# Three edits joined: the opening's group products, the index page transfers and samples' scores, and the last norm

## The reference

```
h = rmsnorm(x, g) * (1 + scale) + shift          # shift, scale, gate = silu(c) @ W + b
x = x + gate * f(h)
```

```
diff = mean_w(h) - h ;  f(h) = (diff @ w_grp[g]) * scale      # w_grp[g] is 256 x 256
```

## Time and profile before

| | us |
|---|---|
| three timed runs | 2660.32, 2654.61, 2649.01 |
| median | 2654.61 |
| the profiled execution, its own time | 2652.98 |
| its span in the trace | 2651.3 |
| busy: TensorE | 2385.3 (90%) |
| busy: VectorE | 1169.5 (44%) |
| busy: ScalarE | 679.7 (26%) |
| busy: GpSimd | 612.6 (23%) |
| opening | 0 to 166.4 |
| first FFN | 166.4 to 947.6 |
| attention input up to the end of the scores | 947.6 to 1134.4 |
| top-k search to second FFN | 1134.4 to 2612.8 |
| last norm | 2612.8 to 2651.3 |

### The profile page before, as it was taken

The page is one execution under the profiler, slowest core; times in us unless marked ns, Lnnn a source line. Parts: engine busy times, 40 slices in busy tenths (PEclk is TensorE's granted clock), DMA queues, the critical chain, the costliest instruction groups (busy, mean ns, idle before and its releaser), DMA issues. The chain is left out here.

```text
span 2651.3 us, 39897 instructions
## 1 busy us (share of the span) xinstructions
PE 2385.3 (90%) x14954; PEld 2064.6 (78%) x14954; DVE 1169.5 (44%) x2611; ACT 679.7 (26%) x1182; POOL 612.6 (23%) x447
## 2 busy tenths in 40 slices
PE   3589999999999998599979995688999999999994
PEld 2569999999999964166634442387999999999994
DVE  6746333333333352478737641233733333333336
ACT  2233111111111042478247761122311111111101
POOL 3602112222222004210036653130222222211210
PEclk8789999999999999799979997789999999999997
DMA  9441111111111032063130008611111111111101
GB/s 397 171 165 48 48 48 47 47 47 47 47 47 47 0 125 87 27 224 99 37 106 21 13 1 281 232 64 48 49 48 48 47 47 47 47 47 47 47 0 65
DMA packets 65631, 206.56 MB, mean 78 GB/s; under 512 B 9572, under 2 KB 28548, under 8 KB 52996
## 3 DMA queue, kind: packets, MB, share of 16 engines
q1 hardware_dynamic: 55184, 183.20, 18.8%
q0 software_dynamic: 7920, 21.22, 2.4%
q10 hardware_dynamic: 2436, 0.92, 0.2%
HBM read 188.52 MB, written 16.13 MB: 77 GB/s over the span
## 5 line engine op out<-in xcount | busy, mean ns | idle before, releaser
L736 PE MATMUL ps<-f_hhi,f_whi 128*128 128x352 f32 x2112 | 682.6, 323 | 3.8 <-DVE f_hlo L295 3.6
L737 PE MATMUL ps<-f_hhi,f_wlo 128*128 128x352 f32 x2112 | 676.8, 320 | 0.0
L738 PE MATMUL ps<-f_hlo,f_whi 128*128 128x352 f32 x2112 | 676.5, 320 | 0.0
L706 POOL TENSOR_TENSOR f_wlo<-f_raw,f_whi 128x2048 fp32r<-128x2048 f32 x62 | 285.2, 4603 | 1224.8 <-ACT f_whi L665 1040.9
L80 DVE SCALAR_TENSOR_TENSOR xT<-ps,mod,xT 128x352 f32<-128x352 f32 (+1 forms) x576 | 327.9, 572 | 214.8 <-PE ps L758 121.4
L736 PEld LDWEIGHTS ps<-f_hhi,f_whi 128*128 128x128 f32 x2112 | 396.1, 188 | 7.9 <-DVE f_hlo L295 6.5
L737 PEld LDWEIGHTS ps<-f_hhi,f_wlo 128*128 128x128 f32 x2112 | 396.9, 188 | 0.0
L738 PEld LDWEIGHTS ps<-f_hlo,f_whi 128*128 128x128 f32 x2112 | 395.9, 187 | 0.0
L756 PE MATMUL ps<-f_ahi,f_whi 128*128 128x352 f32 x1056 | 340.6, 323 | 0.0
L757 PE MATMUL ps<-f_ahi,f_wlo 128*128 128x352 f32 x1056 | 338.3, 320 | 0.0
L758 PE MATMUL ps<-f_alo,f_whi 128*128 128x352 f32 x1056 | 338.1, 320 | 0.0
(11 more groups left out here) (315 smaller groups left out, 2892.9 us busy)
## 6 DMA issues: line engine op xcount, KB each, us to landing
f_raw<-in_ffn SPq DMA_DIRECT2D x66, 1024.0 KB, 4.8
ada_raw<-in_ada SPq DMA_DIRECT2D x18, 2048.0 KB, 11.7
sa_kv<-in_ckv POOLq DMA_DIRECT2D x54, 256.0 KB, 4.5
xT<-in_ada SPq DMA_DIRECT2D x12, 1024.0 KB, 5.3
sa_kv<-in_ckv SPq DMA_DIRECT2D x42, 256.0 KB, 4.7
ai_w<-in_win SPq DMA_DIRECT2D x9, 1024.0 KB, 7.0
xT<-in_ckv SPq DMA_DIRECT2D x23, 256.0 KB, 2.7
xT<-in_xT SPq DMA_DIRECT2D x8, 528.0 KB, 11.0
```

Source lines behind the costliest of these rows:

```text
L706: pool.tensor_tensor(wlo[:, a, :], raw[:, a % 2, :], whi[:, a, :].bitcast(F32), ALU.subtract).then_inc(w_lo, 1)
L736: pe.matmul(c.ps[:, bank, 0:CH], hi[:, k, side, :], hhi[:, k, col], start=(k == 0), stop=False)
L737: pe.matmul(c.ps[:, bank, 0:CH], lo[:, k, side, :], hhi[:, k, col], start=False, stop=False)
L738: last = pe.matmul(c.ps[:, bank, 0:CH], hi[:, k, side, :], hlo[:, k, col], start=False, stop=(k == KD - 1))
```

## The change

Three edits, independent of each other in the code.

1. **Opening.** The mixing products take the plain fp32 weights and differences: two products per bank instead of six, and no rounding and no low halves (`whi`, `wlo`, `dhi`, `dlo` are gone). `df` holds all eight tiles, of the prompt alone. GpSimd makes the samples' differences into `fs`, both tiles of a group in one instruction; TensorE mixes them after the fourth group in 16 products of 32 columns into bank 0, and VectorE adds them in one step for all tiles. `between` becomes [6, 7], [8 to 10], [11, 12], [13 to 17]. Variance, root and reciprocal go by chunk. GpSimd loads `invc` and `vec` first and waits for the last x tile before it issues the other loads; VectorE waits for each table separately.
2. **Index pages and samples' scores.** `load_index_pages` is written out: two page numbers are read, then two DMAs issued, with places in SBUF fixed at build time. SyncE takes parts 0, 2 and 4; GpSimd 1, 3 and 5, all before its small transfers; ScalarE 6 and 7, four pages after each of the evacuations n = 4 to 11, and then the three weight loads. The samples' scores come one at a time after chosen pairs of heads. VectorE's use of the small transfers moves to the last head of block i = 1.
3. **Last norm.** Squares, sums, variance, root and reciprocal by chunk, as in the attention input stage; VectorE makes six y tiles per chunk, GpSimd two (the product with g ahead, then the one with the inverse root); nine stores instead of eight.

The diff, cut to its core:

```diff
 def front_phase
-        between = [range(6, 7), range(7, 9), range(9, 12), range(12, 15), range(15, NQ)]
+        between = [range(6, 8), range(8, 11), range(11, 13), range(13, NQ)]
 ...
 scalar:
-            norm.act_std(act)
-            act.wait_ge(raw_ready, 16)
-            act.activation(whi[:, :], raw[:, :], ACT.Copy).then_inc(w_hi, 1)
+            for ch in range(NCH):
+                act.wait_ge(norm.var_ready, ch + 1)
+                act.activation(norm.rstd[:, cols(ch)], norm.rstd[:, cols(ch)], ACT.Sqrt).then_inc(norm.std_ready, 1)
 ...
-                    if j >= 2:
-                        act.wait_ge(mixed, 6 * g)
-                    act.wait_ge(s_diff, g + 1)
-                    act.wait_ge(scaled, j + 1)
-                    act.activation(dhi[:, j % 2, :], f, ACT.Copy).then_inc(d_hi, 1)
+                    act.activation(df[:, j, 0:SEQ], df[:, j, 0:SEQ], ACT.Copy, scale=c.mod[:, 0, KD + j, 0:1]).then_inc(scaled, 1)
 gpsimd:
+            pool.dma_start(c.invc[:], d.invc).then_inc(invc_ready, 16)
+            pool.dma_start(c.vec[:], d.vec).then_inc(vec_ready, 16)
+            pool.wait_ge(x_ready[KD - 1], 16)
 ...
-                for j in (2 * g, 2 * g + 1):
-                    pool.wait_ge(d_hi, j + 1)
-                    pool.tensor_tensor(dlo[:, j % 2, :], df[:, j % DF, :], dhi[:, j % 2, :].bitcast(F32), ALU.subtract).then_inc(d_lo, 1)
 tensor:
-                            pe.matmul(c.ps[:, q, 0:CH], hi[:, g, k, w], dhi[:, k, col], start=(k == 0), stop=False)
-                            pe.matmul(c.ps[:, q, 0:CH], lo[:, g, k, w], dhi[:, k, col], start=False, stop=False)
-                            last = pe.matmul(c.ps[:, q, 0:CH], hi[:, g, k, w], dlo[:, k, col], start=False, stop=(k == 1))
+                            last = pe.matmul(c.ps[:, q, 0:width(ch)], w[:, g, k, m * P:(m + 1) * P], df[:, 2 * g + k, prompt(ch)], start=(k == 0), stop=(k == 1))
+                if g == 3:
+                    pe.wait_ge(s_diff, 1)
+                    pe.wait_ge(added, 19)
+                    for j in range(KD):
+                        h, m = divmod(j, 2)
+                        for k in range(2):
+                            last = pe.matmul(c.ps[:, 0, NS * j:NS * (j + 1)], w[:, h, k, m * P:(m + 1) * P], fs[:, 2 * h + k].rearrange("p b t -> p (b t)"), start=(k == 0), stop=(k == 1))
+                    last.then_inc(s_mixed, 1)
 vector: (differences 0 to 3, modulation(0), differences 4 and 5, residuals(0), 6, residuals(1), 7, then)
+            residuals(2)
 ...
             modulation(1)
-            residuals(2)
             residuals(3)
+            sample_residuals()

 def load_index_pages
-    with pool.Fori((part % 2) * PAGES // 2, (part % 2 + 1) * PAGES // 2) as i:
-        for half in range(2):
-            page = pool.value_load(c.ptab[0:1, bass.ds(i + (2 * two + half) * PAGES, 1)], min_val=0, max_val=d.n_pages - 1)
-            pool.dma_start(...)
+    for n in range(first, last, 2):
+        i = (part % 2) * PAGES // 2 + n // 2
+        pages = [eng.value_load(...) for half in range(2)]
+        for half in range(2):
+            eng.dma_start(...)

 def attention_input_phase
-        between = [[], [0, 1], [2, 3], [4], [5, 6], [7, 8, 9]]
+        between = {(2, 0): 0, (2, 2): 1, (3, 0): 2, (3, 2): 3, (4, 0): 4, (4, 1): 5, (4, 2): 6, (5, 0): 7, (5, 1): 8, (5, 2): 9}
 sync:
-            sp.wait_ge(ready, EARLY)
-            for u in range(3, 6):
-                sp.dma_start(w[:, u % 3, :], d.win[ORDER[u]]).then_inc(w_ready[u % 3], 16)
-            for p in (4, 6, 7):
-                load_index_pages(sp, c, d, p, page_sp[1])
+            load_index_pages(sp, c, d, 4, page_sp[1])
 gpsimd:
+            load_index_pages(pool, c, d, 5, page_pool[1])      # ahead of the small transfers
 scalar, after evacuation n:
+                if n >= 4:
+                    for p in range(2):
+                        load_index_pages(act, c, d, 6 + p, page_act, max(PAGES // 4 * (n - 4) - PAGES * p, 0), min(PAGES // 4 * (n - 3) - PAGES * p, PAGES))
+            for u in range(3, 6):
+                act.dma_start(w[:, u % 3, :], d.win[ORDER[u]]).then_inc(w_ready[u % 3], 16)
 vector:
-                    if i == 1 and hd == 3:
+                    if i == 1 and hd == NIH - 1:
                         dve.wait_ge(smp_ready, 16 * 14)

 def final_phase
+        @block.gpsimd
+            for i in range(PT):                                 # PT = 2
+                pool.tensor_scalar(xg[:, i, :], c.xT[:, DT + i, :], c.vec[:, g0 + DT + i:g0 + DT + i + 1], None, ALU.mult).then_inc(g_ready, 1)
+            for ch in range(NCH):
+                pool.wait_ge(rstd_ready, ch + 1)
+                for i in range(PT):
+                    pool.tensor_tensor(y[:, DT + i, cols(ch)], xg[:, i, cols(ch)], rstd[:, cols(ch)], ALU.mult).then_inc(y_pool, 1)
 vector:
+            variance(0)
+            invert(0)
+            for ch in range(NCH):
+                tiles(ch, 0, 3)
+                if ch < 2:
+                    variance(ch + 1)
+                tiles(ch, 3, DT)                                # DT = 6
+                if ch < 2:
+                    invert(ch + 1)
```

More of the change, by code:

```diff
@@ L554, in link, with invert @@
                 dve.wait_ge(step, n[0])
+            def invert(ch):
+                dve.wait_ge(norm.std_ready, ch + 1)
+                dve.reciprocal(norm.rstd[:, cols(ch)], norm.rstd[:, cols(ch)]).then_inc(norm.rstd_ready, 1)
             def modulation(s):
@@ L1141, in _ @@
                     pe.matmul(c.ps[:, 2 * (n % 2) + a, 0:wd], qi[rows, j, BLK[i] * P:(BLK[i] + 1) * P], kst[rows, k0:k0 + wd], start=True, stop=True).then_inc(s_ready, 1)
[L1142 to L1144 removed]
+                if (i, j) in between and k0 + wd == widths[i]:
+                    sample_scores(between[i, j])
             head_sum(2 * (SKC + 1) - 1)
@@ L1960, in _, with squares, std @@
         @block.scalar
         def _(act):
-            norm.act_squares(act)
-            norm.act_std(act)
+            def squares(first, last):
+                for n in range(first, last):
+                    ch, j = divmod(n, KD)
+                    if n >= RING:
+                        act.wait_ge(sq_used, n - RING + 1)
+                    act.activation(sq[:, n % RING, :], c.xT[:, j, cols(ch)], ACT.Square).then_inc(sq_ready, 1)
+            def std(ch):
+                act.wait_ge(var_ready, ch + 1)
+                act.activation(rstd[:, cols(ch)], rstd[:, cols(ch)], ACT.Sqrt).then_inc(std_ready, 1)
@@ L1965, in _ @@
+            squares(0, KD + 2)
+            std(0)
+            squares(KD + 2, 2 * KD)
+            std(1)
+            squares(2 * KD, 3 * KD)
+            std(2)
         @block.tensor
         def _(pe):
-            norm.pe_sums(pe)
+            for n in range(NCH * KD):
+                ch, j = divmod(n, KD)
+                pe.wait_ge(sq_ready, n + 1)
+                last = pe.matmul(c.ps[:, 5 + ch, 0:CH], c.ones[:, :], sq[:, n % RING, :], start=(j == 0), stop=(j == KD - 1))
+                last.then_inc(sq_used, 1)
@@ L1969, in _, with variance @@
         @block.vector
         def _(dve):
-            norm.dve_add(dve)
-            norm.dve_rstd(dve)
-            g0 = SUBS * MT + SUBS * KD + KD
-            for j in range(KD):
-                dve.scalar_tensor_tensor(out=y[:, j, :], in0=c.xT[:, j, :], scalar=c.vec[:, g0 + j:g0 + j + 1], in1=norm.rstd[:, :],
-                                         op0=ALU.mult, op1=ALU.mult).then_inc(y_ready, 1)
+            def variance(ch):
+                dve.wait_ge(sq_used, KD * (ch + 1))
+                dve.tensor_scalar(rstd[:, cols(ch)], c.ps[:, 5 + ch, 0:CH], 1.0 / D, EPS, ALU.mult, ALU.add).then_inc(var_ready, 1)
@@ new lines, in invert, with tiles @@
+            def invert(ch):
+                dve.wait_ge(std_ready, ch + 1)
+                dve.reciprocal(rstd[:, cols(ch)], rstd[:, cols(ch)]).then_inc(rstd_ready, 1)
+                dve.wait_ge(rstd_ready, ch + 1)
+            def tiles(ch, first, last):
+                for j in range(first, last):
+                    dve.scalar_tensor_tensor(out=y[:, j, cols(ch)], in0=c.xT[:, j, cols(ch)], scalar=c.vec[:, g0 + j:g0 + j + 1], in1=rstd[:, cols(ch)],
+                                             op0=ALU.mult, op1=ALU.mult).then_inc(y_dve, 1)
```

173 lines of the change are left out of this document (96 added, 77 removed).

## The result

The changed kernel takes 2594.85 us (median of four runs, 2589.45 to 2598.54) against 2654.04 for the kernel before; the ratio is 0.9777, 95% interval 0.9764 to 0.9789. The forecast was 2602.5 in a range of 2582 to 2621. Of the 52 us that it named, 24 + 22 + 6, the two profiles show 29.2 in the opening, 22.9 in the attention input stage up to the first count of the search, and 3.5 in the last norm; 3.7 more lie in stages that nobody touched.

A forecast was written before the change was run, and what follows sets the result against it. Waits other than TensorE's work bound three stages: low halves and modulation loads, index pages, a whole-width last norm. Gains of 24 + 22 + 6 = 52 us from the 2654.61 median gave 2602.5, range 2582 to 2621.

The forecast's parts named there:

- First group: Opening, first mixing group: 12 plain fp32 products, four at the low clock and eight at full, 9.8 us, ending at 66.6.
- VectorE late for the second group: Opening: VectorE's two differences and first residuals end at 68 to 79 beside GpSimd's sample windows; taken as 76.
- Rival C: Opening: VectorE, shut out by GpSimd, holds the banks and each group starts cold; gain 13, time 2613 us; chance 0.12.
- Groups three and four: Opening, third and fourth mixing groups: 8.3 us each, between 7.1 at full clock and 9.8 from a cold start.
- the ring: Opening: three slots for modulation blocks; using a block frees its slot, the load is used 7.7 us later, the next 5.3 later.
- The earlier norm in the opening: Opening: loads behind the last x tile and a norm in three chunks let the first scaling begin earlier; gain 1.9 us.
- The ends of the opening's term: Opening: best and worst cases around the gain of 24 us, given as 33 and 13.
- The pages: Attention input stage: TensorE's 22.6 us hole, waiting for index pages, goes; less 8.7, plus 3.3 and 5, 22 saved.
- The loss at the first score: Attention input stage: GpSimd's small transfers, now behind 48 pages, are done at 1058, delaying the first samples' score by 8.7 us.
- The 5 from spreading the scores: Attention input stage: samples' scores spread over the heads fill TensorE's waits for the relu; 5 us, between 0 and 8.5.
- rivals B and D: B: page issues stay dear on ScalarE and GpSimd, 2616, chance 0.13; D: ScalarE's issues delay attention input, 2669, 0.05.
- The last norm: Last norm by chunk, VectorE and GpSimd excluding each other, 4.8 us a chunk: 6 us saved, 11 without exclusion.

## Why the prediction was right

It held because the three gates that it named were the three that opened: GpSimd's low halves, the index pages, the norm over all columns. Its terms, one by one:

- **First group.** Forecast to end at 66.6, ended at 65.9; the start at the lower clock was right (8.73 for 9.8; 9.85 and 9.97 in the two runs with other places for the blocks).
- **VectorE late for the second group.** The group was forecast to start at 76 and started at 72.95. The size was off: beside GpSimd's sample windows the two differences took 16.5 us (54.90 to 71.38), where the forecast had them and the first residuals at 21.5 and the differences alone at 13.8. Rival C's wait was 1.7 us.
- **Groups three and four.** Costed at 8.3, between a warm and a cold start; they ran at 7.15, full clock, as TensorE now stood 1.66 at most. With the step above and shorter steps between the groups (1.3; the second group and the samples' products took 1.2 more than forecast) that is the 5.5 us by which the whole chain came early: samples done at 116.4 (forecast 122), last block at 131.8 (137.1), first square of the FFN at 137.3 (142.8). The steps between these, 15.4 and 5.5, were as forecast (15.1 and 5.7), and the placing of blocks, tried both ways, bears the ring out.
- **The earlier norm in the opening** (loads behind the x tiles, and chunks) was costed at 1.9, and ScalarE's first scaling began 1.6 earlier (54.84 for 56.47). The chunks have no part in it: with the norm whole again the fourth difference still ended at 50.9, 4.4 earlier than in the kernel before, and VectorE stood. That leaves the order of the loads, which no run shows alone.
- **The ends of the opening's term** are wrong sums: by the steps named they come to 31 and 11, not 33 and 13. The range given hardly depends on it.
- **The pages.** The sum of 22 against 22.9 hides two wrong terms of opposite sign, and luck with the clock. The stage's length depends on the level at which its norm starts, and the kernel before and the changed one started it at different levels (the first row of its products of squares took 6.18 and 7.88; the rows stand below). Like with like, the gain is 26.6 with a first row of 6.18 (187.6 before, 161.0 in the run with the opening of before) and 25.3 with 7.88 (190.0 in the run with the pages of before, 164.7). The loss at the first score was mis-sized: 1.4 to 1.6 instead of 8.7 (from the first square, 101.9 before and 103.5; 103.7 and 105.2). GpSimd's page cost 1.165, not 1.3, and the small transfers began only 1.4 to 1.5 later than before. The 5 from spreading the scores was wrong: nothing to 1.4. With the hole and the 3.3 for VectorE's four heads, which no run shows alone, the sum becomes 22.6 - 1.6 + 3.3 + 1.4 = 25.7, against 26.6.
- **Page issues on ScalarE** (rivals B and D): 4.8 to 5.2 a slot instead of 5.7; scoring started when TensorE's projections ended, and the rivals fell on that price.
- **The last norm.** Forecast first product 9.06 after the first square: it is 10.78 in the changed kernel's profile and 9.06 in the run with the opening of before (2586.50 to 2595.56), which took 32.1, a gain of 6.3. So 6 was right for a norm at full clock, exclusion of GpSimd included (4.5 a chunk for 4.8), and the profile of the result lost 2.8 to the clock.

What the forecast left out altogether is the same clock in the stages that it called unchanged. The second FFN's norm, in the kernel before and after:

```profile
1832.00:1840.00 8.00, 8.00 (x19) 4.80 (x20) 0.53 (x1) 5.01 (x10) 0.00 (x0) 0.67 0.69 262
```

```profile
1779.00:1787.00 8.00, 7.59 (x25) 4.61 (x26) 2.50 (x2) 7.59 (x17) 0.00 (x0) 1.00 0.68 263
```

The same eight us from about the first product of squares on, clock 0.67 and 1.00: the 2.9 us less of that stage. It took 778.7 to 779.3 in nine of the thirteen profiles and 781.7 to 782.0 in four, among them the run with the last norm of before, with all else as in the changed kernel; so here it goes by the run and not by the change. In the attention input stage it doesn't look so: the first row of its norm took 7.88 in all eleven profiles with the changed opening and 6.18 in the two with the opening of before. The kernel before and the changed one:

```profile
948.24 6.18 PE L1047 MATMUL ps<-ai_rel,ones 128*128 128x352 f32 x20 [3.03 <-ACT ai_rel L1167]
```

```profile
919.20 7.88 PE L1055 MATMUL ps<-ai_rel,ones 128*128 128x352 f32 x20 [3.02 <-ACT ai_rel L1175]
```

What decides the level was not tried.

## What to carry to other kernels

When a stage pauses, price the pause twice: the wait itself, and the slower products behind it (3.7 us of wait were worth 7.3 here). A transfer that something waits for should not be issued right behind megabytes that nobody needs yet, and a second engine that shares VectorE's operands is help only if the first doesn't stand for it: measure the engine alone. A right sum is no proof of its terms; undoing one part at a time shows which were right.

## What the runs showed of the hardware

- A transfer of 0.1 to 32 KB landed in 1.6 to 2.2 us alone and in 6.8 to 7.8 beside three loads of 1 MB on another engine's queue. The Trainium skill, "DMA: Bandwidth & Descriptors", section "Queues, rings and completion order", says that a DMA engine takes its queue rows in turn, a packet at a time. The trace agrees in so far as the first small transfer, issued 1.4 us after the last of the three loads, landed at 1016.3, 4.0 before that load; it puts the price of the sharing at 5 us.
- A register-addressed page issue, written out, costs 1.165 us on GpSimd, 1.26 on SyncE, and on ScalarE 1.1 to 1.2 (an evacuation with four, less 0.46).
- The first row of a norm's products, the same twenty records behind a pause of 2.1 to 3.4 us, took 6.18 us (granted clock 1.00) or 7.88 (0.78) in the last norm and in the attention input stage, and 6.18 or 8.9 to 9.2 in the norm of the second FFN.
